# Two output projections of a float32 kernel: two 256-column matmuls joined into one of 512, and the copy-out moved from ScalarE to VectorE

## The reference

```python
def second_block(x, ...):
    for layer in range(2):
        h = rmsnorm_2(x, norm_gains[layer])
        if layer % 2 == 0:
            x = x + even_layer(h, ...)   # ends in concat(...) @ l0_w_out   ("wb" in the kernel)
        else:
            x = x + odd_layer(h, ...)    # ends in concat(...) @ l1_w_out   ("wc" in the kernel)
    return rmsnorm_2(x, final_norm_gain)
```

## Time and profile before

| | |
|---|---|
| median of 3 runs | 2312.03 us (2311.73 to 2314.94) |
| profiled execution: span | 2318.6 us |
| TensorE / VectorE / ScalarE busy | 2075.4 / 1248.6 / 867.8 us |
| mean granted TensorE clock | 0.985 of full |
| "wb" outputs | about 1711 to 1811 us |
| "wc" outputs | about 2203 to 2306 us |
| the three matmul forms of L1260 | 2000 instructions each, 587.2, 569.7 and 569.2 us busy |

### The profile page before, as it was taken

One profiled execution on the slowest core, in us unless ns is written; L12 is line 12 of the kernel. 1 busy time (PEld: TensorE's weight loads), 2 busy tenths in 40 slices (PEclk: granted clock), 3 DMA queues, 4 the chain that ended last, 5 costly groups with the idle time before them and its releaser, 6 DMA issues.

```text
span 2318.6 us, 38453 instructions
## 1 busy us (share of the span) xinstructions
PE 2075.4 (90%) x14546; PEld 1353.4 (58%) x14546; DVE 1248.6 (54%) x2271; ACT 867.8 (37%) x1329; POOL 55.0 (2%) x56
## 2 busy tenths in 40 slices
PE   5899998999988888888888888899999999999998
PEld 2577767772222222222222222699899999998898
DVE  3456567545544444444444444668766564468655
ACT  3333344441111111111111111556756544466654
POOL 0000000000000000000000000110100000011000
PEclk9999999999999999999999999899999999999999
DMA  9998987789999999999999999554445555553443
GB/s 359 356 357 285 316 291 241 283 318 388 428 428 428 427 427 428 428 428 428 428 427 427 427 428 428 216 183 149 146 141 179 181 173 183 181 156 122 141 124 113
DMA packets 135191, 695.43 MB, mean 300 GB/s; under 512 B 15008, under 2 KB 15136, under 8 KB 85408
## 3 DMA queue, kind: packets, MB, share of 16 engines
q1 hardware_dynamic: 135072, 693.79, 78.4%
HBM read 691.63 MB, written 2.10 MB: 299 GB/s over the span
## 4 chain that ended last, share of the span: by engine, by line
PE 48%; DMA 34%; DVE 8%; ACT 4%; SPq 3%; issue 2%; DVEq 0%; ACTq 0%
PE acc L1260 31%; DMA ring<-in_w 29%; DMA land<-in_stream_a 4%; PE psS L1528 3%; PE psO L1319 3%; PE acc L1257 2%; DVE WL L2015 2%; SPq L1075 2%; ACT WH L1696 2%; PE acc L1128 1%; PE psM L1128 1%; DMA land<-in_stream_bc 1%; PE psS L1260 1%; PE psO L1199 1%; PE psT L1191 1%
## 5 line engine op out<-in xcount | busy, mean ns | idle before, releaser
L2015 DVE TENSOR_TENSOR WL<-land,WH 128x1024 fp32r<-128x1024 f32 (+2 forms) x346 | 416.8, 1206 | 397.1 <-ACT WH L1696 392.8
L1260 PE MATMUL acc<-HH,WH 128*128 128x256 f32 x2000 | 587.2, 294 | 4.0 <-DVE HL L2034 2.2
L1260 PE MATMUL acc<-HH,WL 128*128 128x256 f32 x2000 | 569.7, 285 | 0.0
L1260 PE MATMUL acc<-HL,WH 128*128 128x256 f32 x2000 | 569.2, 285 | 0.0
L1696 ACT ACTIVATE WH<-land 128x1024 fp32r<-128x1024 f32 (+2 forms) x350 | 362.4, 1037 | 213.7 <-PE acc L1260 157.7
L1260 PEld LDWEIGHTS acc<-HH,WH 128*128 128x128 f32 x2000 | 387.8, 194 | 26.1 <-issue 12.6
L1260 PEld LDWEIGHTS acc<-HH,WL 128*128 128x128 f32 x2000 | 388.0, 194 | 2.7 <-issue 2.0
L1260 PEld LDWEIGHTS acc<-HL,WH 128*128 128x128 f32 x2000 | 387.4, 194 | 0.0
L1528 PE MATMUL psS<-ring,low 128*32 128x512 f32 x2048 | 274.4, 608 | 99.9 <-DMA ring<-in_w 98.1
L1528 PEld LDWEIGHTS psS<-ring,low 128*32 128x32 f32 x2048 | 40.8, 108 | 310.6 <-DMA ring<-in_w 278.9
L1857 ACT ACT_TABLE_LOAD x32 | 41.1, 1283 | 443.0 <-PE psS L1528 443.0
(11 more groups left out here) (425 smaller groups left out, 2611.9 us busy)
## 6 DMA issues: line engine op xcount, KB each, us to landing
ring<-in_w SPq DMA_DIRECT2D x384, 1024.0 KB, 26.0
land<-in_stream_a SPq DMA_DIRECT2D x284, 512.0 KB, 7.6
land<-in_stream_bc SPq DMA_DIRECT2D x246, 512.0 KB, 4.1
land<-in_stream_bc SPq DMA_DIRECT2D x12, 384.0 KB, 3.7
X<-in_xT SPq DMA_DIRECT2D x1, 2048.0 KB, 14.8
out<-low SPq DMA_DIRECT2D x3, 512.0 KB, 2.7
cst<-in_const SPq DMA_DIRECT2D x1, 1514.5 KB, 10.6
low<-in_w_pool SPq DMA_DIRECT2D x1, 1024.0 KB, 8.3
```

Source lines behind the costliest of these rows:

```text
L1260: mm = pe.matmul(bank[:, 0:S], w[:, kk, :], h[rows[kk]], start=(z == 0 and i == 0), stop=stop)
L2015: ins = dve.tensor_tensor(wl, src, wh, ALU.subtract)
```

## The change

In "wb" and "wc" the high weights are multiplied with high and low tokens in one matmul of 512 columns: the moving operand is a view that holds both (`mix_pair`), and the result fills the whole PSUM bank, WH x HH in one half and WH x HL in the other. WL x HH goes into the first half as before. The two halves of the bank are no longer summed by TensorE: VectorE adds each of them to X, two additions of 256 columns straight from PSUM. ScalarE's copy and VectorE's addition of the copy are gone for these 32 outputs. For the joint view, the tiles HH and HL become the two halves of one tile HX, at the same addresses.

```diff
 def evac_by(x):
-    return "dve" if x[0] in ("bk", "p") or x == LAST_OUT else "act"
+    return "dve" if x[0] in ("bk", "p", "wb", "wc") else "act"
...
         if post == "res":
-            if x != LAST_OUT:
+            if x[0] not in ("wb", "wc"):
                 self.add("dve", "res", x)
...
+        def mix_pair(k, name, c):
+
+            if name == "wb":
+                hi, lo = MIX_HI[c // 4] + c % 4, MIX_LO[c // 4] + c % 4
+                return lowR[:, min(hi, lo):max(hi, lo) + 1:abs(hi - lo), :]
+            return HXs[k][:, :, c, :]
...
+                if name in ("wb", "wc"):
+                    for kk in range(len(rows)):
+                        if n == 0 and kk % 4 == 0:
+                            needs(k, "dve", o, "ml", name, rows[kk] // 4)
+                        pe.matmul(bank[:, :].rearrange("p (z s) -> p z s", z=2), wh[:, kk, :], mix_pair(k, name, rows[kk]),
+                                  start=(i == 0 and kk == 0), stop=False, skip_group_check=True)
+                        mm = pe.matmul(bank[:, 0:S], wl[:, kk, :], HH[rows[kk]], start=False,
+                                       stop=(last and kk == len(rows) - 1), skip_group_check=True)
+                    mm.then_inc(done[k]["pe"], 1)
+                    return
...
-                        if name == "wc":
+                        if name in ("wb", "wc"):
+                            then(dve.tensor_tensor(X[:, n, :], X[:, n, :], bank[:, S:2 * S], ALU.add))
                             ins = dve.tensor_tensor(X[:, n, :], X[:, n, :], bank[:, 0:S], ALU.add)
```

More of the change, by code:

```diff
@@ L855, in program @@
         WLs = [inside(f"WL{k}", [P, PARTS, HALF], F32R, parts_at[k] + 4 * PARTS) for k in range(2)]
-        HHs = [inside(f"HH{k}", [P, KD, S], F32R, parts_at[k] + 8 * PARTS) for k in range(2)]
-        HLs = [inside(f"HL{k}", [P, KD, S], F32R, parts_at[k] + 8 * PARTS + KD) for k in range(2)]
+        HXs = [inside(f"HX{k}", [P, 2, KD, S], F32R, parts_at[k] + 8 * PARTS) for k in range(2)]
+        HHs, HLs = ([h[:, z, :, :] for h in HXs] for z in range(2))
         land = [inside(f"land{k}", [P, LAND[k], HALF], F32, 0) for k in range(2)]
@@ L917, in program @@
         cDQ, cDK = 16, 24
-        dRT, dT2, dTM, dSQ, dSA, dKX = 58, 59, 60, 62, 64, 66
+        dRT, dT2, dSQ, dSA, dKX = 58, 59, 62, 64, 66
         dV, dRQ, dVE = 51, 52, 53
@@ L1251, in product @@
                             needs(k, "dve", o, "cl", *(("cq", kk) if name == "qr" else ("ckv", kk)))
-                        if x in (("wp", 0), ("wo", 0), ("wb", 0), ("wc", 0)) and term == 0 and kk % 4 == 0:
-                            needs(k, "dve", o, "ml", "wo" if name == "wp" else name, rows[kk] // 4)
+                        if x in (("wp", 0), ("wo", 0)) and term == 0 and kk % 4 == 0:
+                            needs(k, "dve", o, "ml", "wo", rows[kk] // 4)
                         stop = last and z == len(terms) - 1
@@ L1627, in evac @@
                         return act.activation(W(MIX + 8 + c)[:, 0, :], a, ACT.Copy, scale=C("pool_scale", c, 1))
-                    if name in ("wp", "wo", "wb", "wc"):
+                    if name in ("wp", "wo"):
                         if n >= 2:
@@ L1634, in evac @@
                             needs("dve", "res", ("wp", n + KD - 2))
[L1635 to L1638, removed]
+                        return act.activation(W(aTM + n % 2)[:, 0, :], a, ACT.Copy, scale=gt1[:, n:n + 1])
                     if name == "h2t":
@@ L1706, in run @@
                         else:
-                            needs("dve", "res", (name, 4 * (c // 8) + c % 4 if name == "moe" else c))
+                            needs("dve", *(("evac", (name, c)) if name == "wb" else ("res", (name, 4 * (c // 8) + c % 4))))
                             if name == "wb" and c == 0:
@@ L1768, in run @@
                         n = x[1]
-                        needs("dve", "evac" if x == LAST_OUT else "res", x)
+                        needs("dve", "evac" if x[0] in ("wb", "wc") else "res", x)
                         sq = W((aSQ if k == 0 else dSQ) + n % 2)[:, 0, :]
@@ L1780, in run @@
                         n = step[1]
-                        needs("dve", *(("evac", LAST_OUT) if n == KD - 1 else ("res", ("wc", n))))
+                        needs("dve", "evac", ("wc", n))
                         ins = act.activation(W(MIX + n)[:, 0, :], X[:, n, :], ACT.Copy, scale=C("gain_f", n, 1))
@@ L2168, in run @@
                             needs("act", "evac", step[1])
-                            tm = W((aTM if k == 0 else dTM) + n % 2)[:, 0, :]
+                            tm = W(aTM + n % 2)[:, 0, :]
                             ins = dve.tensor_tensor(X[:, n, :], X[:, n, :], tm, ALU.add)
@@ L2210, in run @@
                         needs("pe", "proj", x)
-                        bank = acc[o.acc.index(("proj", x)) % 2]
+                        bank = (*bankS, psM[:, :])[SPARE[x]] if x in SPARE else acc[o.acc.index(("proj", x)) % 2]
                         if name == "p":
```

## The result

| | before | after |
|---|---|---|
| median | 2312.78 us (2311.73 to 2314.94, 4 runs) | 2325.60 us (2321.31 to 2326.13, 4 runs) |
| ratio to before | | 1.0041 (95% interval 1.0027 to 1.0055) |
| profiled span | 2318.6 us | 2324.2 us |
| mean granted TensorE clock | 0.985 | 0.985 |

The change makes the kernel slower, by 9.5 us by the ratio and 12.8 by the medians; forecast were 10.4 us and a time of 2322.4, with a range of 2317.5 to 2326.0. As a difference the forecast of 10.4 us lies between the two ratios (9.5 and 12 us); as a time, 2322.4 us is 3.2 us under the median.

What follows compares the result with a forecast made beforehand. TensorE was taken as the bound (5.76 us per output), the VectorE-ScalarE circle just under it; the change makes the circle the bound. 5.2 + 0.8 + 4.4 = +10.4 us on 2312.0 gives 2322.4 us, range 2317.5 to 2326.0.

Steps and rivals of the forecast that it cites:

- The circle: "wb" and "wc": VectorE addition, ScalarE square and split, VectorE low part, next addition; second addition +0.46 us per output.
- TensorE: Joined matmuls in "wb" and "wc": 5.55 us per output instead of 5.76, work down 6.7 us, hidden.
- The upper bound for 512 columns: Joined matmul in both projections: at most 430 ns, the time read for plain float32; 227 taken.
- rival D: The 512-column matmul is slow, 430 ns: an output takes 8.8 us, total 2410; chance 2%.
- "wb" to "cq" 0: From "wb" to the end of "cq" 0: VectorE's delay, 6.4 less 0.5 us, holds up the token split; +5.2 us.
- The clock: Two TensorE waits around the end of "wb" may lower the clock; half of up to 1.6 us taken, +0.8.
- "wc": From "wc" to the end: nine long rounds and one short, plus the second addition in the tail; +4.4 us.
- Middle: From "cq" on to "wc": nothing changed, TensorE sets the pace, the earlier delay is carried on whole.
- Rival A: "wb" and "wc": second addition costs nothing in the round, TensorE stays the bound, faster, 2309.8 us; chance 3%.
- Rival B: PSUM addition at 0.35 or a later stage giving back "wb" delay, no clock loss: 6.5 us, or 2316.2; chance 7%.
- Rival C: TensorE's waits of about 0.5 us per output hold it at 1.2 GHz half the time: 2358 us; chance 4%.

Runs made afterwards that it cites:

- e3: Changed kernel with ScalarE's weight split moved ahead of square and gain in "wb" and "wc": 2307.18 us, ratio 0.9972 to before.
- e1: The changed kernel run again, unaltered: 2325.57 us, ratio 1.0052 to before.
- e2: Changed kernel with the joined matmul undone (three matmuls of 256 columns), the two VectorE additions kept: 2324.78 us, ratio 1.0053 to before.
- e6: The change made in projection "wb" alone, "wc" as before: ratio 1.0021 to before, 4.9 us.
- e7: The change made in projection "wc" alone, "wb" as before: ratio 1.0019 to before, 4.4 us.
- e5: Changed kernel without the second VectorE addition, one bank half left out of X: 2309.99 us, ratio 0.9987 to before.
- e4: Kernel before the change with ScalarE's weight split moved ahead of square and gain: 2312.64 us, ratio 0.9995 to before.

## Why the prediction was right

- *The circle.* Forecast 6.08 and 6.10 us per output, measured 6.07 and 6.09. The second addition was priced at 0.46 and took 0.45. Its duration was taken from the one row of its shape, not from the wider one, and that held. That ScalarE's lost copy gives back nothing held too (idle 2.08 to 2.95).
- *TensorE.* Forecast 0.227 us for a matmul of 512 columns and 5.55 us for an output. Where nothing hides it, in e3, a pair takes 0.351 to 0.353 us, so the matmul 0.351 - 0.119 = 0.232 to 0.353 - 0.120 = 0.233, and an output 5.62 to 5.65. That is midway between the two cases that were weighed, 0.227 (the excess over the column time belongs to the instruction) and 0.240 (to the columns), so neither is shown. TensorE's work falls by 0.08 to 0.11 us per output, not by 0.21: some 3 us in all, not 6.7. The term was too large by half and did no harm, because the circle hides it.
- *The spacing rule.* With the spacing rule of the Trainium skill (TensorE: Matmul & The Clock Gate, "Back-to-back issue gap"; columns / 2.4 + 2.5 ns) a pair would take 0.325 us, by estimate. The section gives this rule for isolated matmuls and says that in a stream of weight loads and matmuls it is too high at 512 columns, which the prediction left out. Here such a stream takes more than the rule, 0.351 to 0.353 us for a pair.
- *Plain float32.* The prediction read 0.215 and 0.430 us as the time of a plain float32 matmul of 256 and of 512 columns. They are records, and the profile shows two for each such matmul: one step of L1505 has two matmuls and makes four records. A whole one takes 0.43 and 0.86 us. The upper bound for 512 columns and the price of rival D should have been about twice as high; the forecast doesn't use them.
- *"wb" to "cq" 0.* Forecast +5.2 us. Measured to the end of the second "cq" output: +5.6. The pattern at the end is the one forecast: TensorE waits for a low weight part, then for the token split.

```profile
1809.11 0.35 PE L1277 MATMUL acc<-HX,WH 128*128 128x256 f32 x1 [1.20 <-DVE WL L2029]
1813.39 0.39 PE L1277 MATMUL acc<-HX,WH 128*128 128x256 f32 x1 [1.55 <-DVE HX L2042]
```

- *The clock.* The step that failed: +0.8 us for a fall of the clock after these two waits. It measured 0. TensorE by stretch (columns as in the earlier trace rows) shows 1.00 right through them:

```profile
1706.00:1730.00 24.00, 21.62 (x126) 1.00 0.48 152
1808.00:1820.00 12.00, 9.23 (x73) 1.00 0.54 166
2226.00:2232.00 6.00, 5.43 (x31) 1.00 0.00 0
```

  All four kernels that have these two waits (after, e1, e2, e6) pass them at 1.00. The same rows show that even the wait of 2.4 us at the head of "wb", after which the clock was 0.79 before, passed without a fall this time, and so did the one at the head of "wc". A fall seen in one profile was no ground for a charge on a new wait, nor for counting on the old one.
- *What a fall costs.* It depends on who sets the pace, which the prediction did not ask. In e6 the clock was 0.50 in the head of the changed "wb", and the stage took 113.28 us, against 113.25 after, where it did not fall. In e1 it fell in "wc", after two waits for a low weight part that the changed kernel has there (1.25 and 1.77 us; before, one of 0.72), and the stage took 111.41 us against 111.55. TensorE in e6, then in e1 (columns as in the earlier trace rows):

```profile
1727.50:1730.90 3.40, 3.40 (x13) 0.50 0.05 17
2252.30:2255.70 3.40, 3.40 (x11) 0.50 0.68 213
```

- *"wc".* Forecast +4.4, measured +3.75 in the profiles. The execution of before had lost up to 1.35 us to a slower clock in the head of "wc" (its first finishing half took 4.25 us where 24 matmuls take 2.9), and the one after had not. Against a before without this fall the price would be up to 5.1, an estimate. "wb" before had its fall too; how much of it reached the end of the stage no run shows.
- *Middle.* Forecast 0, measured +0.9 us between two executions whose clocks differed there (0.94 and 0.89). e6 and e7 together make what the whole costs, so no third place with a price of its own is seen.
- The sum, +10.3 by the stages against +10.4, is nearer than its terms, and that is luck: "wb" came out 0.4 over and the middle 0.9 over its forecast, the clock term 0.8 and "wc" 0.65 under. What is right beyond luck is the round of the circle, and with it the direction and the size of each stage's loss.

Rival A (TensorE stays the bound) fell with the first round read; e5 shows what it would have been, 0.9987. Rival B (partly absorbed) is out in its first part, since the second addition took 0.45 us and not 0.35; whether some tenths of the "wb" delay are given back later stays open (e6). Rival C (the clock falls in the circle) fell with the clock of 1.00 in both middle stretches, in which TensorE had 0.45 us less work than time in every output (6.07 - 5.62). The one fall, in e1, came at longer waits, where the head of "wc" ends, and did not come back in the rounds behind it. The swinging clock that the Trainium skill describes (TensorE: Matmul & The Clock Gate, "A second HAM failure mode: psum-queue depth-cycling") did not show in these stretches, at idle shares of 7%. Rival D fell at 0.23 us per joined matmul.

## What to carry to other kernels

When two engines at 60% busy each idle for the other in every round, add up the round (from one instruction to its next occurrence): if it is close to the time of the engine that seems to be the bound, the spare capacity is not there, and an instruction of 0.45 us put into the round costs 0.45 us each time, however small the engine's share. Before moving work off the bound, look at which instruction in the round waits only because of its place in an in-order list (here a weight split behind a square); moving that first turned a loss of 0.4 to 0.5% into a gain of 0.3%.

## What the runs showed of the hardware

- A float32r matmul of 128 x 128 weights with 256 columns is spaced 0.119 to 0.120 us (e4) and one of 512 columns 0.232 to 0.233 us (e3) at 2.4 GHz, so joining two saves 0.005 to 0.007 us, 2 to 3%.
- The profile has two records for a plain float32 matmul, of 0.215 us each at 256 columns and 0.430 at 512 (before, L1505 and L1199).
- TensorE can look full and not be: in the middle of "wb", after, its records cover 60.53 of 60.67 us, with 56.2 us of work in them at the spacing of e3.
- VectorE's float32 addition of 128 x 256 takes 0.42 us with one operand from PSUM and with both from SBUF alike.
- After a wait of TensorE of 2.2 us at the same place in the program, the granted clock over 30 us was 0.94 in some kernels and 1.00 in others (2210 to 2240 us: 0.94 before, in e2, e4 and e6; 1.00 after and in e1, e3, e5, e7). Where TensorE is on the path, such a fall cost up to 1.35 us (before, head of "wc"), as much as some of the effects looked for here; where the circle set the pace, it cost nothing that shows (e6 in "wb", e1 in "wc").
